# One engine for all evictions of a transposed half, later expert loads, and a separate row buffer for the last tile

## What is computed

```python
def conformer_conv(h, w1, b1, dw_w, dw_b, ln_g, ln_b, w2, b2):
    z = jax.nn.glu(h @ w1 + b1, axis=-1)
    z = causal_dw_conv(z, dw_w) + dw_b
    z = jax.nn.silu(layer_norm(z, ln_g, ln_b))
    return z @ w2 + b2
...
    a = jax.nn.silu(jnp.einsum('td,edf->tef', t, w_gate)) * jnp.einsum('td,edf->tef', t, w_up)
    y = jnp.einsum('tef,efd->td', a * gates[:, :, None], w_down)
...
def reference(x, c, ...):
    for l in range(DEPTH):
        h = modulate(rms_norm(x, norm_mix_g[l]), sh1, sc1)
        y = hybrid_ab(h, ...) if l % 2 == 0 else conformer_conv(h, ...)
        x = x + g1[:, None, :] * y
        h = modulate(rms_norm(x, norm_ffn_g[l]), sh2, sc2)
        x = x + g2[:, None, :] * grouped_moe(h, ...)
    return rms_norm(x, final_norm_g)
```

## Time and profile before

| | |
|---|---|
| three runs | 1672.8, 1674.31, 1677.0 us, median 1674.31 |
| the profiled execution | 1671.73 us, its span 1669.9 us |
| busy | PE 1544.7 us (92%), DVE 821.9 (49%), ACT 266.7 (16%), POOL 246.1 (15%) |
| chain that ended last | PE 74%, DVE 14%, DMA 6% |
| granted TensorE clock, mean | 0.974 of full speed |

### The profile page before, as it was taken

How to read it: one execution, slowest core, us unless ns; L and a number is a source line. 1 busy time by engine, 2 the same in 40 slices (tenths; PEclk the granted TensorE clock), 3 DMA queues, 4 the chain that set the end, 5 groups by cost and what they waited for, 6 DMA issues and landing times.

```text
span 1669.9 us, 17355 instructions
## 1 busy us (share of the span) xinstructions
PE 1544.7 (92%) x5589; PEld 844.7 (51%) x5590; DVE 821.9 (49%) x1584; ACT 266.7 (16%) x526; POOL 246.1 (15%) x412
## 2 busy tenths in 40 slices
PE   5989999999998999999896999999899899999991
PEld 3764544447884444444443434345588444444440
DVE  2463587654326223223227798999543622322323
ACT  3200000000212111111130000012241211111112
POOL 2000000000001232322200000313000122332220
PEclk9999999999999999999998999999899999999996
DMA  9644057643118788898474454454111989778846
GB/s 334 202 146 159 26 160 249 208 128 124 51 76 301 253 262 228 237 320 245 75 240 114 112 143 120 114 146 111 55 51 76 345 268 342 184 208 262 251 88 226
DMA packets 201459, 302.41 MB, mean 181 GB/s; under 512 B 10517, under 2 KB 160113, under 8 KB 201408
## 3 DMA queue, kind: packets, MB, share of 16 engines
q1 hardware_dynamic: 179040, 222.71, 41.9%
q0 software_dynamic: 18800, 65.39, 15.8%
q10 hardware_dynamic: 3568, 13.63, 2.1%
HBM read 248.55 MB, written 53.10 MB: 181 GB/s over the span
## 4 chain that ended last, share of the span: by engine, by line
PE 74%; DVE 14%; DMA 6%; SPq 2%; issue 2%; ACT 1%; POOL 0%; POOLq 0%; DVEq 0%; ACTq 0%
PE bank L1139 19%; PE bank L990 19%; PE bank L1069 16%; PE bank L1154 10%; DVE R L1770 7%; DVE WX L1350 3%; PE bank L1121 2%; DMA xsum_scratch<-R,TSUM 2%; PE bank L1251 1%; SPq L462 1%; PE bank L1086 1%; DMA WX<-in_ada_w 1%; PE bank L973 1%; PE bank L1007 1%; SPq L463 1%
## 5 line engine op out<-in xcount | busy, mean ns | idle before, releaser
L990 PE MATMUL bank<-HTR,WX 128*128 128x512 f32 x1024 | 453.0, 599 | 6.0 <-DMA WX<-in_hyb_w_in 5.1
L1139 PE MATMUL bank<-WX,R 128*128 x784 | 346.5, 595 | 4.3 <-DMA WX<-in_moe_w_gate 2.3
L990 PEld LDWEIGHTS bank<-HTR,WX 128*128 128x128 f32 x1024 | 192.7, 191 | 245.5 <-issue 238.5
L1770 DVE SCALAR_TENSOR_TENSOR R<-R,PT 128x512 f32<-128x512 f32 (+18 forms) x288 | 231.2, 803 | 10.2
L1069 PE MATMUL bank<-WX,R 128*128 128x256 f32 x1024 | 230.5, 384 | 2.2 <-DVE R L1327 1.1
L1139 PEld LDWEIGHTS bank<-WX,R 128*128 128x128 f32 x784 | 145.7, 191 | 170.0 <-issue 170.0
L1327 DVE TENSOR_TENSOR R<-bank,R 128x256 f32<-128x256 f32 (+2 forms) x77 | 38.8, 504 | 366.9 <-ACT R L744 255.8
L1069 PEld LDWEIGHTS bank<-WX,R 128*128 128x128 f32 x1024 | 194.3, 192 | 31.6 <-issue 2.7
L1154 PE MATMUL bank<-WX,R 128*128 x408 | 183.8, 593 | 4.1 <-DVE R L1592 4.1
L1350 DVE SCALAR_TENSOR_TENSOR WX<-WX,CAB 128x256 f32<-128x256 f32 x280 | 135.8, 485 | 10.0
L1599 DVE SCALAR_TENSOR_TENSOR R<-bank,GSLOT,HTR 128x512 f32<-128x512 f32 x51 | 38.3, 751 | 166.5 <-DMA xsum_scratch<-R,TSUM 111.8
(11 more groups left out here) (212 smaller groups left out, 1082.5 us busy)
## 6 DMA issues: line engine op xcount, KB each, us to landing
WX<-in_ada_w SPq DMA_DIRECT2D x48, 1024.0 KB, 11.8
WX<-in_moe_w_gate SPq DMA_DIRECT2D x32, 1024.0 KB, 7.1
WX<-in_moe_w_up SPq DMA_DIRECT2D x32, 1024.0 KB, 12.3
WX<-in_moe_w_down SPq DMA_DIRECT2D x32, 1024.0 KB, 15.3
WX<-in_conf_w SPq DMA_DIRECT2D x20, 1024.0 KB, 9.3
WX<-glu_scratch SPq DMA_DIRECT2D x64, 260.0 KB, 4.5
WX<-in_hyb_w_in SPq DMA_DIRECT2D x10, 1024.0 KB, 12.0
xsum_scratch<-WX ACTq DMA_DIRECT2D x8, 1024.0 KB, 4.0
```

What stands on the lines that cost most here:

```text
L990: ins = pe.matmul(dst[:], lhs(k), rhs(k), start=(k == 0), stop=(k == kc - 1))
L1139: ins = pe.matmul(M[0][:], XT[:, k, :], WX[:, bass.ds(at + k * 2 * FE, 2 * FE)], start=(k == 0), stop=(k == KC - 1))
L1770: link(dve.scalar_tensor_tensor(out=o[:, t0:HT], in0=p[:, HT * h + t0 - d:HT * h + HT - d], scalar=tap(CTAPS - 1 - d), in1=o[:, t0:HT], op ...
```

## The change

Three things are changed.

1. ScalarE evicts all eight blocks of the second half of Layer 1 (its `evict_ht` gets a list of blocks `ks`, takes bank `TB_[k % 2]` and counts on the semaphore that TensorE waits for). VectorE's part of it at n == 2 is gone.
2. SP loads expert 0 as before, then waits for the first gather (`xg_in[l]`) before it loads expert 1. The wait for `xpj` before expert 2 is gone. Experts 2 and 3 follow at once.
3. The output rows of a layer's last tile go to a buffer of their own, `YL`. VectorE no longer waits for the rows of the tile before to be stored. POOL's `add_last` copies the token numbers to `TCUR` once the last gather has landed, and waits for the store of the tile before only ahead of its own transfer.

```diff
@@ -229,6 +229,7 @@
         XG = R[:, 1, 0:D]
         XT = R[:, 1, D:2 * D].rearrange("p (k t) -> p k t", k=KC)
         YS = R[:, 1, 2 * D:3 * D]
+        YL = R[:, 0, 0:D]
         SG = R[:, 1, 3 * D:3 * D + FE]
         AG = R[:, 1, 3 * D + FE:3 * D + 2 * FE]
         AT = R[:, 1, 3 * D + 2 * FE:3 * D + 3 * FE].rearrange("p (k t) -> p k t", k=2)
@@ -304,8 +305,8 @@
         xn_ok = sem("xn_ready")
         xn_out = [sem(f"xn_stored{n}") for n in range(2)]
         tr = sem("xn_transposed")
-        tev_a = sem("ht_evicted_by_act")
-        tev_d = sem("ht_evicted_by_dve")
+        tev_a = sem("ht_even_evicted")
+        tev_d = sem("ht_odd_evicted")
         full = sem("main_bank_full")
         free = {"A": sem("main_bank_emptied_by_act"), "D": sem("main_bank_emptied_by_dve")}
         ln_var = sem("ln_variance_ready")
@@ -464,8 +465,8 @@
 
             def experts(l):
                 for e in range(NEB - 1):
-                    if e == NEB - 2:
-                        sp.wait_ge(xpj, 16 * (l + 1))
+                    if e == 1:
+                        sp.wait_ge(xg_in[l], 16)
                     expert(l, e, e)
 
                 sp.wait_ge(xg_in[l], 16)
@@ -642,9 +643,23 @@
                     pool.wait_ge(sum_cur[l], t + 1)
                     pool.wait_ge(ys_d[l], t + 2)
                     met()
+                    send(TSUM, YS)
+
+                def add_last(t):
+
+                    pool.wait_ge(xg_in[l], t * 16 + 32)
+                    pool.tensor_copy(TCUR[:], TOKI[:, bass.ds(t, 1)]).then_inc(sum_cur[l], 1)
+                    pool.wait_ge(sum_cur[l], t + 1)
+                    pool.wait_ge(ys_d[l], t + 2)
+                    pool.wait_ge(y_out[l], t * 16 + 16)
+                    met()
+                    send(TCUR, YL)
+
+                def send(tokens, y):
+
                     pool.indirect_dma_start(
-                        out=xs_dram, out_offset=bass.IndirectOffsetOnAxis(ap=TSUM[:, 0:1], axis=0),
-                        in_=YS, in_offset=None, compute_op=ALU.add).then_inc(y_out[l], 16)
+                        out=xs_dram, out_offset=bass.IndirectOffsetOnAxis(ap=tokens[:, 0:1], axis=0),
+                        in_=y, in_offset=None, compute_op=ALU.add).then_inc(y_out[l], 16)
 
                 met()
                 pool.wait_ge(tok_ok, l + 1)
@@ -660,8 +675,7 @@
                     next_tile(t + 2)
                     add_rows(t)
                 add_rows(more)
-                add_rows(more + 1)
-                pool.wait_ge(xg_in[l], more * 16 + 48)
+                add_last(more + 1)
                 if l == 0:
                     pool.wait_ge(tapc_in, 16 * SH * SH)
                     pool.wait_ge(quads_ok, 1)
@@ -710,14 +724,14 @@
                 s = slice(4 * h, 4 * h + 4)
                 act.activation(SD[:, s], SS[:, s], ACT.Sqrt, bias=EPSC[:], scale=1.0 / D).then_inc(rms_sd, 1)
 
-            def evict_ht(r, l, ffn, h, beside=lambda k: None):
-                for k in range(0, KC, 2):
+            def evict_ht(r, l, ffn, h, beside=lambda k: None, ks=range(0, KC, 2)):
+                for k in ks:
                     beside(k)
                     act.wait_ge(tr, 8 * r + 8 * h + k + 1)
                     act.wait_ge(ada_fin, k + 2 if r == 0 else NADA)
-                    act.activation(HTR[:, k, HT * h:HT * h + HT], TB_[0][:], ACT.Identity,
+                    act.activation(HTR[:, k, HT * h:HT * h + HT], TB_[k % 2][:], ACT.Identity,
                                    bias=MC[:, l, 2 * ffn + 1, k:k + 1],
-                                   scale=MC[:, l, 2 * ffn, k:k + 1]).then_inc(tev_a, 1)
+                                   scale=MC[:, l, 2 * ffn, k:k + 1]).then_inc((tev_a, tev_d)[k % 2], 1)
 
             def take(g):
                 act.wait_ge(full, g + 1)
@@ -862,7 +876,7 @@
             act.dma_start(B2B, on_all(i["conf_b2"][0], D)).then_inc(gb_in[2], 16)
             for n in range(NSTEP):
                 if n == 2:
-                    evict_ht(2, 1, 0, 1)
+                    evict_ht(2, 1, 0, 1, ks=range(KC))
                 gate1(n)
                 if n == 10:
                     quarters_out(0, 0)
@@ -1595,10 +1609,14 @@
 
                     dve.wait_ge(dn[l], t + 1)
                     dve.wait_ge(y_out[l], t * 16 + 16)
+                    rows_by(t, YS)
+
+                def rows_by(t, y):
+
                     g = GSLOT[:, bass.ds(t, 1)]
-                    dve.scalar_tensor_tensor(out=YS[:, 0:HT], in0=M[1][:], scalar=g, in1=GBF[:, 0:HT],
+                    dve.scalar_tensor_tensor(out=y[:, 0:HT], in0=M[1][:], scalar=g, in1=GBF[:, 0:HT],
                                              op0=ALU.mult, op1=ALU.mult)
-                    dve.scalar_tensor_tensor(out=YS[:, HT:D], in0=M[2][:], scalar=g, in1=GBF[:, HT:D],
+                    dve.scalar_tensor_tensor(out=y[:, HT:D], in0=M[2][:], scalar=g, in1=GBF[:, HT:D],
                                              op0=ALU.mult, op1=ALU.mult).then_inc(ys_d[l], 1)
                 hidden(0)
                 turned(0)
@@ -1606,7 +1624,8 @@
                     hidden(t)
                     tile_out(t - 1)
                     turned(t)
-                tile_out(nt - 1)
+                dve.wait_ge(dn[l], nt)
+                rows_by(nt - 1, YL)
 
             def last_norm(b):
 
@@ -1786,8 +1805,6 @@
             for n in range(NSTEP):
                 c, h = w1_group(n)
                 g = GROUPS["w1"] + 2 * n + 1
-                if n == 2:
-                    evict_ht(2, 1, 0, 1)
                 dve.wait_ge(free["A"], emptied(g - 1))
                 dve.scalar_tensor_tensor(out=GT[:, c, HT * h:HT * h + HT], in0=take(g)[:],
                                          scalar=PT[:, COL_B1 + c:COL_B1 + c + 1],
```

## The result

The changed kernel took 1654.4 us (median of four runs, 1653.3 to 1656.7) against 1673.55 for the kernel before beside it (1672.6 to 1677.0): a ratio of 0.989 with an interval of 0.987 to 0.991. The forecast was 1656.3 with a range of 1652.5 to 1663. The profiled execution took 1653.37, its span went from 1669.9 to 1651.5.

What follows compares the result with a forecast made beforehand. TensorE was taken to bound the kernel, standing still mainly in the second half's transposes behind VectorE's queue. Gains of 14.5 + 3.0 + 0.5 = 18.0 us took 1674.31 to 1656.3 us, range 1652.5 to 1663.

Steps and rivals of the forecast that it cites:

- The bound: Whole kernel: TensorE is three quarters of the chain, so only its stand-still or shorter stretches between its stages pay.
- Part 1, 14.5 us: Second half's transposes in Layer 1: step 2's products start at 899.3 to 899.4 instead of 913.94; bounds 13.4 and 14.7.
- Case (c): Later w1 steps: something TensorE overtook holds it, half of the 14.5 us is lost, 1663.5 us; chance 0.05.
- The rule weighed: Second half's transposes: the skill says transposes don't count for the clock gate, so products could start at 1.2 GHz.
- case (d): Step 2's first products: the clock is down at 899, costing 1.7 us, so 1658 us; chance 0.05.
- Part 3, 3.0 us: End of each layer's MoE: the last addition of rows is issued 1.5 us earlier per layer; bounds 2.6 and 3.4.
- Part 2, 0.5 us: Layer 1's MoE start: the first gather lands in 4.1 us in quiet queues, removing TensorE's 0.56 us idle time.
- The 1.7 us that I had left to the range: Layer 1's second product: 7.13 instead of 8.83 us if the clock stays up; counted in the range only.
- (a): Each MoE's start: expert 1 lands late, 3.7 us in Layer 0, 3.2 in Layer 1; 1659 to 1667 us; chance 0.13.
- (b): Layer 1's first five experts: loads at 16.3 us each make expert 5 19.3 us late, 1682 us; chance 0.03.
- How long does a load take from a standing start?: Expert 1's load behind the first gather: taken as 14 us, 16.3 from expert 4; hidden with 0 to 3 us to spare.
- The sum: Whole kernel: 14.5 + 3.0 + 0.5 = 18.0 us gained, from a median of 1674.31 to 1656.3 us.

Runs made afterwards that it cites:

- the doubled evictions: The changed kernel with the first six ScalarE evictions of the second half done twice, the first time into unused space; ratio 0.9951 to the kernel before.
- part 3 alone: The kernel before with only the last tile's rows given a buffer of their own; ratio 1.0006 (0.9995 to 1.0016).
- e1_early: The changed kernel with expert 1 loaded at once again and only experts 2 and 3 behind the first gather; ratio 0.9889 to the kernel before.
- the two later issues: The changed kernel with loads of experts 1 to 3 held until tile 0 was transposed (1658.15 us), or until the second gather had landed (1667.45 us).
- The three parts alone: Each of the three changes by itself on the kernel before: ScalarE evictions 0.9918, later expert loads 0.9989, the last tile's own buffer 1.0006.

## Why the prediction was right, and which steps of it were not

**The bound: right.** It was idle time of TensorE that went; neither VectorE nor ScalarE took its place.

**Part 1, 14.5 us: right, 14.9 measured.** The pace of ScalarE was the term that was off. The prediction took 0.78 + 0.03 = 0.81 us per eviction, from one eviction with a handoff on each side. Eight back to back take 6.02 us, first to last, 0.75 each, and the doubled ones 0.66: the 0.78 us of one overlap with the next. The measured 14.9 lies 0.2 us beyond the high bound of 14.7. That VectorE would wait about 4.8 us and not be in the way was right (4.5), and so was that all of it reaches the end: the stage behind it is 406.50 against 406.63, and 406.1 to 407.7 in the other executions with part 1, the doubled evictions left out. Case (c) fell.

**The rule weighed, case (d): fell here.** Between 893.4 and 899.1 TensorE did transposes alone, with a granted clock of 1.00, and the 32 matmuls of the product after took 13.90 us against the 13.93 of a later step. By the rule of the Trainium skill (TensorE: Matmul & The Clock Gate, Part 4, PE-mode transpose) they could have started at the lower clock; this stretch doesn't agree. (The records show them as matmuls with the identity; whether the mode that the page means is on, no run here shows.) Another stretch of the changed kernel doesn't agree either. At 855.12, after 4.26 us of idle time, TensorE starts on transposes alone, and the granted clock rises among them:

```profile
855.90:856.70 0.80, 0.80 (x6) 0.72 (x4) 0.00 (x0) 0.49 (x1) 0.00 (x0) 0.50 1.02 405
...
860.50:861.50 1.00, 0.75 (x6) 0.50 (x6) 0.81 (x1) 0.25 (x2) 0.00 (x0) 1.00 0.12 7
```

The doubled evictions show the opposite, a clock that falls among transposes with longer gaps (0.68 to 1.10 us). So the disagreement holds for these stretches and not for every run of transposes.

**Part 3, 3.0 us: under half of it by the stages, nothing by the whole runs of part 3 alone.** The additions lie 1.4 and 1.5 us closer, as worked out. In Layer 1 that reached the end in this execution, and not in the next one of the same kernel (7.92 us apart). The prediction took the last product's 3.7 us as given; the old wait would have covered a slower one. In Layer 0 the step that failed is "TensorE's warming matmuls start 2.2 us earlier and end at 853.9; the normalised rows come at 854.4 and decide". I moved the block of warming matmuls with its duration of 20.42 us. But that row holds some matmuls at the lower clock (granted 0.50 from 835.6 to 840.0), which follow the idle time of 3.77 us ahead; the 3.0 us more are about seven of them. With 2 us less idle time they all run at the upper clock, the block takes 17.43 us, ends at 850.9, and leaves 4.26 us of idle time, after which the transposes run at the lower clock: 1.1 us lost. The remaining 0.6 us of the 1.7 is the reload (20.57 us from the last addition to the transposes, against 19.95), which varies from 19.7 to 21.5 between executions of the kernels that leave it as it is, and which I don't ascribe. In effect the old wait had been holding the warming back until it fitted.

**Part 2, 0.5 us: not by the way that I gave.** The gather lands in 4.3 us instead of 7.9, as forecast. Yet Layer 1's first transposes come 7.99 us after the gather's issue, and came after 7.87 before: warming matmuls in front of them were still running (until 1313.8, at the lower clock in part). So the term of 0.5 us for a gather that lands sooner was nothing in this execution. Over all profiled executions it is 7.15 to 8.16 us in the nine with part 2 and 7.48 to 7.99 in the four without, because with part 2 the filler decides: its eight matmuls ahead of the last step of the routing took 3.68 us in one execution and 6.25 in another. Up to tile 1's transposes the parts differ more: 17.1 to 18.4 us from the first gather's issue with part 2 (18.24 in the changed kernel) and 18.3 to 19.2 without (18.73 before). `e1_early`, with its gather of 7.5 us, has 17.7, so some tenths of a us are there, and I can't give them to the quiet gather. The 1.7 us that I had left to the range (a second product of 7.13 instead of 8.83) did come in the profiled execution and not in the next one of the same kernel; that it fell into the execution compared is luck.

**Rivals (a) and (b): fell, because one term was too large.** "How long does a load take from a standing start?" I answered 14, with 16.3 as the bound, from expert 4, which had a gather and an addition of rows beside it. Measured are 536.38 + 10.7 - 535.14 = 11.9 us in Layer 0 and 12.8 in Layer 1, each beside one gather, and 12.4 to 13.4 where it was issued later. In Layer 0 the load was done at 547.1, 3.9 us before tile 1 (549.46 + 1.50), and in Layer 1 3.8 us before it, where I gave 0 to 3. It also made my expectations of the two later issues too high, 4 for 5 to 12 and 13 for 22 or more.

**The sum.** 14.5 + 3.0 + 0.5 = 18.0 against 18.4 in the profiled execution. The near agreement is luck in part, since two errors cancel: part 3 gave 1.8 us less than said (1.2 when the reload's 0.6 us are not counted against it), and Layer 1's MoE gave 1.8 us more, of which 1.7 was a matter of the execution. The three parts alone come to 13.7 + 1.8 - 1.0 = 14.5 us by their ratios, each known to 2 or 3 us, against 17.9 by the ratio of the changed kernel. For part 1 and for the end of Layer 0 the short stages are the better ledger.

## What to carry to other kernels

Where an engine stands still, look at what is queued ahead of the operation that releases it. If that is long work which another, idle engine could stand in for, moving the release can be worth nearly the whole idle time, as here. Filler that keeps TensorE's clock up is tuned to the wait that it fills: whoever shortens a chain beside it has to count the filler again, with durations at the clock that it will then run at, not at the one it ran at. A wait that is taken away may have covered the delays of another engine, which then show. And cut both traces at common instructions before explaining a difference of 1%: a total that agrees with the forecast can hide two terms that don't, and only a second execution tells which stages repeat.

## What the runs showed of the hardware that I had not expected

- An idle time of 4.26 us ahead of the transposes cost 1.1 us in the work behind it (7.91 us instead of 6.80, granted clock 0.78 over the stretch), one of 0.61 us nothing. Over fourteen profiled executions it was 7.68 to 8.59 us behind 2.69 us or more and 6.79 to 6.81 behind 1.06 us or less.
- After such an idle time the clock rose while TensorE did transposes alone (granted 0.50 from 855.9 to 858.5, 1.00 from 859.5), and among transposes with gaps of 0.68 to 1.10 us it fell.
- The lower clock comes and goes between executions of one kernel: the second product of Layer 1 took 7.13 us in one and 8.82 in the next, with 0.48 and 0.15 us of idle time ahead of the tile's transposes. A gap's length in one trace didn't explain it, and what does stays open.
- The last addition of 128 rows held the reload back for 6.13 us, and for 8.57 us with two megabytes of loads beside it. The first gather took 4.3 to 4.7 us alone and 7.4 to 7.9 beside queued experts, one expert being enough (7.7). An expert's 3 MB took 11.9 to 13.4 us from a standing start.
- Eight evictions in a row by ScalarE, each recorded with 0.78 us, took 6.02 us together.
